# The last gated-delta head of a one-core decoder step: its row norm, turning and gating moved into the output projections, and the next weights' splits into its scan

## What is computed

```python
h = x + 0.5 * rmsnorm(swiglu(rmsnorm(x)))
u = rmsnorm(h);  proj = u @ w_in
o_a = diff_attention(...)                       # 8 heads of 128
o, S = gated_delta_chunked(q, k, v, g, beta, S0)  # 8 heads of 128
o_b = rmsnorm(o, delta_norm) * silu(z)          # per head and token
merged = sigmoid(gate_a) * (o_a @ w_a_out) + sigmoid(gate_b) * (o_b @ w_b_out)
h = h + rmsnorm(merged @ w_o)
y = h + 0.5 * rmsnorm(swiglu(rmsnorm(h)))
```

## Time and profile before

| | |
|---|---|
| time, median of 3 runs (lowest, highest) | 3777.68 us (3775.6, 3782.03) |
| time of the profiled execution | 3776.84 us |
| its span, first to last instruction | 3775.2 us |
| TensorE matmuls, busy | 3586.6 us (95%) |
| VectorE, ScalarE, GpSimd busy | 1827.1, 1275.9, 595.0 us |
| mean granted clock of TensorE | 0.978 of full speed |

### The profile page before, as it was taken

How to read it: one execution, slowest core, us unless ns; L and a number is a source line. 1 busy time by engine, 2 the same in 40 slices (tenths; PEclk the granted TensorE clock), 3 DMA queues, 4 the chain that set the end, 5 groups by cost and what they waited for, 6 DMA issues and landing times. The chain is left out here.

```text
span 3775.2 us, 63419 instructions
## 1 busy us (share of the span) xinstructions
PE 3586.6 (95%) x24244; PEld 3397.3 (90%) x24244; DVE 1827.1 (48%) x3202; ACT 1275.9 (34%) x2610; POOL 595.0 (16%) x567
## 2 busy tenths in 40 slices
PE   8999999989999999798999999998899999999998
PEld 7999999978889888676899989997899899999997
DVE  4344344374555455443665556566332534434436
ACT  4111111155444445333444443444322611111113
POOL 1000000013111121000332223333001110000001
PEclk9999999999999999898999999999999999999998
DMA  3111111122121222496011111002432321111111
GB/s 96 48 45 46 45 45 46 45 74 63 58 63 57 63 66 94 157 380 210 19 35 41 40 40 35 28 25 76 138 91 74 120 74 50 46 46 45 46 45 58
DMA packets 280232, 271.34 MB, mean 72 GB/s; under 512 B 13988, under 2 KB 221038, under 8 KB 279950
## 3 DMA queue, kind: packets, MB, share of 16 engines
q1 hardware_dynamic: 270550, 236.51, 20.0%
q0 software_dynamic: 9344, 30.88, 2.5%
q10 hardware_dynamic: 84, 0.35, 0.0%
HBM read 223.71 MB, written 43.98 MB: 71 GB/s over the span
## 5 line engine op out<-in xcount | busy, mean ns | idle before, releaser
L2311 PE MATMUL ps<-p_hi,w_hi 128*128 128x352 f32 x2016 | 652.5, 324 | 5.2 <-DVE f_acc L2262 2.9
L2311 PE MATMUL ps<-p_lo,w_hi 128*128 128x352 f32 x2016 | 647.9, 321 | 7.3 <-issue 7.3
L2311 PE MATMUL ps<-p_hi,w_lo 128*128 128x352 f32 x2016 | 647.1, 321 | 0.0
L2311 PEld LDWEIGHTS ps<-p_hi,w_hi 128*128 128x128 f32 x2016 | 379.2, 188 | 7.1 <-DVE f_acc L2262 3.7
L2311 PEld LDWEIGHTS ps<-p_lo,w_hi 128*128 128x128 f32 x2016 | 379.8, 188 | 5.7 <-issue 5.5
L2311 PEld LDWEIGHTS ps<-p_hi,w_lo 128*128 128x128 f32 x2016 | 379.1, 188 | 3.2 <-issue 3.2
L607 PE MATMUL ps<-p_hi,w_hi 128*128 128x352 f32 x912 | 305.1, 335 | 1.2 <-PEq L120 1.2
L607 PE MATMUL ps<-p_hi,w_lo 128*128 128x352 f32 x912 | 293.5, 322 | 0.0
L607 PE MATMUL ps<-p_lo,w_hi 128*128 128x352 f32 x912 | 293.5, 322 | 0.0
L2157 ACT CAST w_hi<-w_raw 128x1024 fp32r<-128x1024 f32 x128 | 133.4, 1042 | 385.6 <-PE ps L2330 385.6
L1809 PE MATMUL ps<-p_hi,w_hi 128*128 128x352 f32 x768 | 256.9, 335 | 0.0
(11 more groups left out here) (492 smaller groups left out, 8058.5 us busy)
## 6 DMA issues: line engine op xcount, KB each, us to landing
w_raw<-in_ffn_w_in_dram SPq DMA_DIRECT2D x88, 512.0 KB, 3.9
w_raw<-in_w_in_dram SPq DMA_DIRECT2D x70, 512.0 KB, 3.9
sa_v<-in_cache_v_dram SPq DMA_DIRECT2D x128, 256.0 KB, 7.3
w_raw<-in_ffn_w_out_dram SPq DMA_DIRECT2D x44, 512.0 KB, 3.7
sa_k<-in_cache_k_dram SPq DMA_DIRECT2D x80, 256.0 KB, 6.3
second<-in_cache_k_dram SPq DMA_DIRECT2D x40, 256.0 KB, 6.0
d_gates<-at_gate POOLq DMA_DIRECT2D x16, 528.0 KB, 5.2
op_gb<-d_gates SPq DMA_DIRECT2D x16, 528.0 KB
```

The lines of the kernel that those rows point to most:

```text
L2311: mm = nc.tensor.matmul(m.ps[:, 3 * g + c, 0:CH], a[:, g, w], x[:, f, cols(c)], start=(f == 0 and n == 0), stop=(f == KT - 1 and n == 2))
```

## The change

The row work of head 7 is taken out of the delta block. Its tiles `ssq`, `orow`, `zs` are placed at addresses that the next block doesn't reuse at once, and the next block does the work beside its first units: one root on ScalarE and one reciprocal and one product of 128x1152 on VectorE at the start, eight transposes behind unit 0 and one behind unit 2 on TensorE (banks 6 and 7), three gating products behind the chunks of units 1 and 2 on VectorE, straight into the staging place of tile 7. Tile 7 is no longer written to `d_ob` and read back. The splits of the first two `w_a_out` tiles move into head 7's scan. The two states of head 7 are written by SyncE instead of GpSimd, and their landing is waited for by SyncE at the start of the next block instead of by GpSimd at the end of this one. Cut to its core, with "..." where lines are left out:

```diff
@@ delta_heads, SyncE: end
+                sp.wait_ge(s_done_s, 2 * H)
+                sp.dma_start(delta_sample.rearrange("o b h k v -> h k (o b) v")[H - 1], sts[:, :, :]).then_inc(m.last_states, 16)
+                sp.wait_ge(s_done, TT * H)
+                sp.dma_start(delta_prompt.rearrange("o b h k v -> (o b h) k v")[H - 1], st[:, :]).then_inc(m.last_states, 16)
@@ delta_heads, ScalarE
+            def next_high(k):
+                act.wait_ge(next_in[k], 16)
+                nc.scalar.copy(m.w_hi[:, k, :], m.w_raw[:, k, :]).then_inc(next_hi, 1)
...
                 if not more:
                     other(6)
+                    next_high(0)
...
                     row_square(t)
+                    if not more and t == 3:
+                        next_high(1)
...
-            def end():
-                out_root(H - 1)
-                for k in range(2):
-                    act.wait_ge(next_in[k], 16)
-                    nc.scalar.copy(m.w_hi[:, k, :], m.w_raw[:, k, :]).then_inc(next_hi, 1)
@@ delta_heads, VectorE, in the scan
+                    if not more:
+                        if t == 1:
+                            next_low(0)
+                        if t == 4:
+                            next_low(1)
+                        if t == 5:
+                            other(7)
...
-            def end():
-                for x in range(3):
-                    row_norm(x, H - 1)
-                next_low(0)
-                for g in range(3):
-                    gate_rows(g, H - 1)
-                next_low(1)
@@ delta_heads, GpSimd
+                if last(h):
+                    return
                 pool.wait_ge(s_done_s, 2 * h + 2)
...
-            schedule(pool, first, head, lambda: store(H - 1))
+            schedule(pool, first, head, lambda: None)
             pool.wait_ge(tail_out, 32 * H)
-            pool.wait_ge(out_done, 16 * H)
-            pool.wait_ge(state_out, 32 * H)
+            pool.wait_ge(out_done, 16 * (H - 1))
+            pool.wait_ge(state_out, 32 * (H - 1))
@@ delta_heads, TensorE
-            def end():
-                pe.wait_ge(s_done_s, 2 * H)
-                for g in range(3):
-                    out_rows(g, H - 1)
@@ outputs_ffn, SyncE
+            sp.wait_ge(m.last_states, 32)
             gate(0)
...
-            for j in range(BUFS, KT):
+            for j in range(BUFS, KT - 1):
                 other(j)
@@ outputs_ffn, ScalarE
             def other(j):
-                act.wait_ge(ob_in[j % BUFS], 16 * (j // BUFS + 1))
+                if j < KT - 1:
+                    act.wait_ge(ob_in[j % BUFS], 16 * (j // BUFS + 1))
+                else:
+                    act.wait_ge(fin_gated, 3)
...
+            nc.scalar.activation(m.fin_ssq[:, 3, :, 1], m.fin_ssq[:, 3, :, 0], ACT.Sqrt, ...).then_inc(fin_root, 1)
@@ outputs_ffn, VectorE
+            def fin_rows(g):
+                a, b = (512 * g, 512 * g + 512) if g < 2 else (LP, T)
+                dve.wait_ge(fin_turned, g + 1)
+                if g == 0:
+                    dve.wait_ge(ob_lo, BUFS)
+                nc.vector.scalar_tensor_tensor(out=staged(KT - 1)[:, a:b], in0=m.ps[:, 6 + g % 2, 0:b - a], ...).then_inc(fin_gated, 1)
+            dve.wait_ge(fin_root, 1)
+            nc.vector.reciprocal(m.fin_ssq[:, 3, :, 1], m.fin_ssq[:, 3, :, 1]).then_inc(fin_scale, 1)
+            dve.wait_ge(fin_scale, 1)
+            nc.vector.tensor_tensor(m.fin_rows[:, :, :], m.fin_rows[:, :, :], ..., ALU.mult).then_inc(fin_normed, 1)
...
+                if n == 1:
+                    fin_rows(0)
+                    fin_rows(1)
+                elif n == 2:
+                    fin_rows(2)
                 low(n + 2)
@@ outputs_ffn, TensorE, in the loop over units n
+                if n == 0:
+                    pe.wait_ge(fin_normed, 1)
+                    fin_turn(0)
+                    fin_turn(1)
+                elif n == 2:
+                    fin_turn(2)
```

More of the change, by code:

```diff
@@ L1093, in delta_heads @@
         kd = sb("kd", [P, NT, P])
-        orow = sb("orow", [P, NT, P])
         bt = sb("bt", [P, NT, 3, P])
@@ L1104, in delta_heads @@
         pp_s = sb("pp_s", [NS, NS])
+        vnt = sb("vnt", [P, 2, NS])
+        wq = sb("wq", [P, NB, 2, LS])
+        ssq = sb("ssq", [P, 4, NT, 2])
+        orow = sb("orow", [P, NT, P])
+        zs = sb("zs", [P, T])
+        m.fin_ssq, m.fin_rows, m.fin_z = ssq, orow, zs
+        pp = sb("pp", [P, 2, 4, P])
         dif = pp[:, 0, :, :]
@@ L1416, in head @@
                     silus(h + 1, 1)
-            def end():
-                out_root(H - 1)
-                for k in range(2):
-                    act.wait_ge(next_in[k], 16)
-                    nc.scalar.copy(m.w_hi[:, k, :], m.w_raw[:, k, :]).then_inc(next_hi, 1)
-            schedule(act, first, head, end)
+            schedule(act, first, head, lambda: None)
         @block.vector
@@ L1686, in head @@
                         nc.vector.tensor_tensor(sts[:, 4 * g:4 * g + 4, :], sts[:, 4 * g:4 * g + 4, :], bank4(3 + 4 * g, 4, P), ALU.add).then_inc(s_done_s, 1)
-                    if not more and t == 5:
-                        other(7)
+                    if not more:
[5 more added lines that the diff above has]
+                            other(7)
                     if more:
@@ L1708, in head @@
                             low(n + 2, k)
-            def end():
-                for x in range(3):
-                    row_norm(x, H - 1)
-                next_low(0)
-                for g in range(3):
-                    gate_rows(g, H - 1)
-                next_low(1)
-            schedule(dve, first, head, end)
+            schedule(dve, first, head, lambda: None)
         @block.gpsimd
@@ L2092, in head @@
                         states(1)
-            def end():
-                pe.wait_ge(s_done_s, 2 * H)
-                for g in range(3):
-                    out_rows(g, H - 1)
-            schedule(pe, first, head, end)
+            schedule(pe, first, head, lambda: None)
 def ffn_units(nc, m, sem, w_in, w_out, hid_hi, hid_lo, first_hi, first_lo, silu, hid, rstd, spans, sq, sq_last, post):
@@ L2872, in outputs_ffn @@
     with ExitStack() as ctx:
-        sem = semaphores(nc, ctx, "op_")
+        sem = semaphores(nc, ctx, "op_", [m.last_states])
         place = lambda to, n, s, d=F32: to.enter_context(nc.sbuf_tensor("op_" + n, s, d))
@@ L2884, in outputs_ffn @@
         stage_in = [sem(f"stage_in{k}") for k in range(3)]
+        fin_root, fin_scale, fin_normed, fin_turned, fin_gated = (sem("fin_" + n) for n in ("root", "scale", "normed", "turned", "gated"))
         HALF = KT // 2
@@ L3138, in merge @@
                 nc.vector.tensor_tensor(m.p_lo[:, f, :], m.acc[:, f, :], m.p_hi[:, f, :].bitcast(F32), ALU.subtract).then_inc(merged_lo, 1)
+            def fin_rows(g):
[3 more added lines that the diff above has]
+                    dve.wait_ge(ob_lo, BUFS)
+                nc.vector.scalar_tensor_tensor(out=staged(KT - 1)[:, a:b], in0=m.ps[:, 6 + g % 2, 0:b - a], scalar=m.gain[:, 6 * KT + 1:6 * KT + 2],
+                                               in1=m.fin_z[:, a:b], op0=ALU.mult, op1=ALU.mult).then_inc(fin_gated, 1)
+            dve.wait_ge(fin_root, 1)
+            nc.vector.reciprocal(m.fin_ssq[:, 3, :, 1], m.fin_ssq[:, 3, :, 1]).then_inc(fin_scale, 1)
+            dve.wait_ge(fin_scale, 1)
+            nc.vector.tensor_tensor(m.fin_rows[:, :, :], m.fin_rows[:, :, :], m.fin_ssq[:, 3, :, 1:2].to_broadcast([P, TT + 1, P]), ALU.mult).then_inc(fin_normed, 1)
             for n in range(A):
@@ L3273, in ffn_first, with fin_turn @@
                 e.first_chunk(pe, c, g)
+            def fin_turn(g):
+                if g == 2:
+                    pe.wait_ge(fin_gated, 1)
+                for j in range(4 if g < 2 else 1):
+                    w = P if g < 2 else NS
+                    mm = nc.tensor.transpose(m.ps[:, 6 + g % 2, j * P:j * P + w], m.fin_rows[0:w, 4 * g + j, :], ident[0:w, 0:w])
+                mm.then_inc(fin_turned, 1)
             for n in range(A):
```

7 lines of the change are left out of this document (2 added, 5 removed).

## The result

The changed kernel takes **3769.94 us** (median of 10 runs, 3761.51 to 3777.7); the kernel before, measured beside it, takes 3777.53 us (10 runs, 3767.21 to 3782.03). The ratio of the two is 0.9978, with a 95% interval of 0.9968 to 0.9988: faster by 8.3 us by this ratio, and by something between 4.5 and 12.1 (the two medians lie 7.6 apart). The profiled execution of the changed kernel took 3771.61 us, its span is 3770.0.

What follows compares the result with a forecast made beforehand. TensorE's chain was taken to bound the kernel, with only the barrier before unit 0 as a wait. 11.25 (border) - 1.0 (transposes) + 1.05 (clock) = 11.3 us gain, so 3777.68 becomes 3766.4 us, range 3762.5 to 3772.

Steps and rivals of the forecast that it cites:

- The tail goes: Border after head 7's scan: only SyncE's two state stores remain; with the scan's growth counted, unit 0 begins 11.25 us earlier.
- The scan grows by the splits: Head 7's scan: first rounding adds 0.99 us, second 0.68, the two VectorE subtractions fit idle time; together 1.67 us.
- two pauses behind the earlier trace: TensorE pauses at 2607.1 to 2609.8 (clock stayed 1.00) and 2613.0 to 2615.4 (then 0.53 for 3.6 us).
- the prediction's own signs of being wrong: Several-microsecond drain at the border; late state updates or more half clock in the scan; TensorE waiting before unit 2 or 3.
- The clock at unit 0: Unit 0's start: a shorter TensorE pause of 2.3 us may keep full clock; gain 0 to 2.1 us, middle 1.05.
- Nine transposes: TensorE beside the first units: nine transposes at 0.11 us apiece cost 1.0 us; other work beside the units costs nothing.
- SyncE's wait for the states: Next block's start: states land about 0.3 us behind the barrier, work queued behind has 9 us to spare; costs nothing.
- B: Head 7's scan pays all four split pieces, 4.4 us instead of 1.67, without clock gain; gain 7.5, 3770.2 us; chance 0.11.
- C: Block's end: SyncE's end waits for landing and drains like GpSimd's, 1.8 + 3.33 us more; 3772.4 us; chance 0.07.
- D: Next block: SyncE's queue, held by the states' wait, delays unit 2; slower, 3783 us if landing takes 25; chance 0.03.
- E: Border: something else holds the barrier to about its old time, so the change doesn't do what it says; chance 0.03.

Runs made afterwards that it cites:

- idle_both: Changed kernel with both weight roundings and the seventh input row's split moved to later places in head 7's scan; 3767.02 us, ratio 0.9966 to the kernel before.
- late_other: Against idle_both, VectorE's split of the attention's sixth tile moved from ahead of the three v products to behind them; 3760.67 us, ratio 0.9951 to the kernel before.
- states_pool: Changed kernel with the last two state stores given back to GpSimd, landing waited for at the block's end; 3775.67 us, ratio 0.9985 to the kernel before.

## Why the prediction was right or wrong

The forecast was 3766.4 us and a gain of 11.3; measured are 3769.94 us and 8.3 (4.5 to 12.1). Inside the profiles, where the spread is less, the gain to the end of unit 2 is 73.54 - 64.48 = 9.1 us, from two profiles before and three after. By its parts:

- **The tail goes**: right. Ahead stood a border of 15.6 us and behind it one of 2.7; it is 2.78. The issue of 0.33, the drain of 0.14 and the 1.36 us to the first matmul came out as 0.34, 0.138 and 1.33. GpSimd's drain lies in the scan and costs nothing.
- **The scan grows by the splits, 1.67 us**: this is the step that failed, by its size. It grew by 5.3, 3.8 and 2.7 us, 3.9 on average, which is more than twice what was put down. The two subtractions cost nothing, as put down. The second rounding was put at 0.68 and costs 0.45. The first was put at 0.99, as the length of the pause it adds, and that the pause is about 1 us longer is right (0.67 to 1.61). What the sum didn't hold is that the longer pause also lets the clock stay at half for 7 to 14 us of the scan instead of 3.7, at 0.36 us for each. Against the 3.9 us of half clock before, this is 1.1 us in the mildest profile and 3.6 in the profiled execution. One of the two pauses behind the earlier trace rows had shown that a pause can do this; they were used for unit 0 alone, and the scan got no clock term. More half clock inside the scan was also one of the prediction's own signs of being wrong, and it came.
- **The clock at unit 0, 1.05 between 0 and 2.1**: right as a mean, and by luck, since no single execution gains it. After the same border unit 0 stayed at full clock in 2 of 9 profiles and takes 11.69 us there. In the other 7 it stood at half for 3.4 us, beginning at once or up to 1.1 us into the unit, and takes 13.3 to 13.4. Before it took 13.82 on average, so the gain is 2.1 or 0.5. The three profiles of the changed kernel give 1.04 on average; over all nine it is 0.9. The two pauses behind the earlier trace rows were not equally near: by TensorE's timeline of the kernel before they are 1.92 and 2.24 us, and the border now has 2.40. But even one length goes both ways. After the pause of 2.24 us the clock fell before; in the changed kernel, in the second row, the same pause stands in a stretch of full clock (1.00 from 2615 to 2629 us).

```profile
2615.47 3.66 PE L1960 MATMUL ps<-dl_uu,dl_mk 128*128 128x128 f32 x16 [2.24 <-DVE dl_uu L1616]
2619.76 1.16 PE L1968 MATMUL ps<-dl_uu,dl_mk 128*128 128x128 f32 x8 [2.24 <-DVE dl_uu L1625]
```

- **Nine transposes, 1.0 us**: measured 1.05. No wait of TensorE stands ahead of them, and the root, the scaling, the gating and the splits beside the units are hidden.
- **SyncE's wait for the states**: nothing, as put down. The store landed in 1.5 us.

With the measured parts the local sum is 12.85 (border) - 3.94 (scan) + 1.04 (clock) - 0.90 (units 1 and 2, now with the eight transposes) = 9.05, the gain that the profiles show. The total's 8.3 can't be split further: its interval is wider than any of these terms but the border.

Of the rivals, **B** was nearest in its number (3770.2) and half right in its reason. It held that all four pieces land on the scan, and half clock besides. The pieces don't, since the subtractions are hidden. Half clock does. The rows it leaned on, don't lie in the scan but over 13 us ahead of it. **C** is refuted: SyncE's drain took 0.138 us and ended before the landing, and with the states stored by GpSimd the border is 5.4 us longer, where the prediction had 5.1 between the two. The Trainium skill ("DMA: Bandwidth & Descriptors", on issuing engines not being separate DMA queues) says that starting transfers from several engines only saves the sequencer's issue time. For the transfer itself the rows are not far from this, 1.5 us to landing from SyncE and 1.8 from GpSimd. But that is not the whole price at the end of a block: there the engine's drain differs too, 3.25 us against 0.14, and in this test the place of the wait for the landing. **D** and **E** did not come.

## What to carry to other kernels

In a chain of short products the price of an added piece is the idle time that it makes ahead of TensorE, and beyond it what the granted clock does in the microseconds behind; look at the clock by stretches there, and put the piece behind the first copy that TensorE waits for instead of ahead of it. Here the same two roundings cost 3.9 us in one place and nothing in another. At the end of a block, let an engine whose drain is short issue the last store, and carry the wait for its landing into the next block, ahead of the first thing that overwrites what it reads.

## What the runs showed of the hardware that was not expected

- The granted clock can stay at 0.50 for 13.7 us with TensorE shown busy in all of them (the second stretch of the changed kernel), after a pause of 1.6 us and with little idle time in between. A small pause thus costs more than its own length. The Trainium skill ("TensorE: Matmul & The Clock Gate", Part 1) says of the slow matmuls at a kernel's start that their count isn't to be fitted, since it differs between runs, and that they cost under 1% of a typical span. In the middle of this kernel both are so too: 7.0 to 14.0 us for the same kernel, and at most 3.6 us of 3770, 0.1%. The change as a whole is worth only 0.22%, so it decided the size of the result anyway.
- A VectorE subtraction of one size took 2.78 us beside a GpSimd product that covered 1.66 us of it, and 1.23 us without one. VectorE in idle_both (the kernel before has the same 2.78 us):

```profile
2624.38 2.78 DVE L1471 TENSOR_TENSOR p_lo<-dl_xc,p_hi 128x1056 fp32r<-128x1056 f32 x1
```

  GpSimd in idle_both:

```profile
2624.15 1.89 POOL L1772 TENSOR_TENSOR dl_tt<-dl_kd,cst 32x1024 f32<-32x1024 f32 x1 [3.13 <-PE ps L1984]
```

  and VectorE in late_other, where it stands behind the products of `v`:

```profile
2623.78 1.23 DVE L1471 TENSOR_TENSOR p_lo<-dl_xc,p_hi 128x1056 fp32r<-128x1056 f32 x1
```

  The Trainium skill ("GPSIMD Engine Reference", "Key points") says that the two engines share their interfaces to the on-chip memory, and that VectorE's instructions with two inputs there contend; these rows agree. In late_other the three products of `v`, which read one input from PSUM (`ps`), stand beside the same GpSimd product instead and take 1.47 us, as long as without it in idle_both. That the contention is the cause was not tested by a run that takes GpSimd's product away.
- GpSimd's drain takes 3.08, 3.25 and 3.33 us (and the rows of the changed kernel and of states_pool above), whether the last store ahead of it is the small one of the convolution rows, a state or the `zs` of a head. So it is a price by itself, and it counts only where it ends last.
- The root follows its table load at once: the load starts at 2665.34 and takes 1.28 us, the root starts at 2666.63. The Trainium skill ("ScalarE: Activation LUTs", "What ACT_TABLE_LOAD costs") adds a drain of about 1.38 us to each switch; none stands between these rows.
